# ScalarE's order inside the mixers' slots: key merges before the output tile, turned-weight copies before the next exponentials

## What is computed

```python
# mixer 1, per head: a chunked scan with decays (forward and backward)
A = jnp.einsum('bhtk,bhsk,bhtsk->bhts', qc, kc, decay)
o = einsum('bhts,bhsv->bhtv', A, vc) + einsum('bhtk,bhkv->bhtv', qc * exp(b), S)
# mixer 2, per head: differential attention over blocks of 128 queries
p = jax.nn.softmax(s, axis=-1)
a = p[:, :, 0] - lam * p[:, :, 1]
return jnp.einsum('bhqk,bhkv->bhqv', a, v)
```

## Time and profile before

| what | value |
|---|---|
| median of 3 runs | 2445.93 us (2445.45 to 2447.43) |
| profiled execution, its own time | 2445.96 us |
| its span | 2444.1 us |
| TensorE busy | 2428.1 us (99%) |
| VectorE busy | 1825.5 us (75%) |
| ScalarE busy | 1302.2 us (53%) |
| mixers of layer 0 and of layer 1 | from 240 to 503 us and from 1451 to 1714 us |

### The profile page before, as it was taken

One profiled execution on the slowest core, in us unless ns is written; L12 is line 12 of the kernel. 1 busy time (PEld: TensorE's weight loads), 2 busy tenths in 40 slices (PEclk: granted clock), 3 DMA queues, 4 the chain that ended last, 5 costly groups with the idle time before them and its releaser, 6 DMA issues.

```text
span 2444.1 us, 40830 instructions
## 1 busy us (share of the span) xinstructions
PE 2428.1 (99%) x16442; PEld 2259.2 (92%) x16442; DVE 1825.5 (75%) x2395; ACT 1302.2 (53%) x2006; POOL 189.3 (8%) x236
## 2 busy tenths in 40 slices
PE   9999999999999999999999999999999999999998
PEld 9999889898999999888899998989989999998887
DVE  6665777754788998978585567776648889999784
ACT  6444666543465555556454456664435565554563
POOL 0001011100200000003110011111002000000031
PEclk9999999999999999999999999999999999999999
DMA  5454444254323333833233544433443222346421
GB/s 177 141 173 142 133 144 134 97 184 152 104 71 90 90 104 105 300 114 128 97 130 124 187 134 140 136 122 123 174 146 110 65 89 83 107 160 247 154 92 61
DMA packets 290267, 321.52 MB, mean 132 GB/s; under 512 B 10400, under 2 KB 223904, under 8 KB 290080
## 3 DMA queue, kind: packets, MB, share of 16 engines
q1 hardware_dynamic: 215744, 171.39, 22.5%
q10 hardware_dynamic: 74336, 147.53, 16.6%
HBM read 253.60 MB, written 65.27 MB: 130 GB/s over the span
## 4 chain that ended last, share of the span: by engine, by line
PE 95%; DVE 2%; ACT 2%; issue 1%; POOL 0%; ACTq 0%; DVEq 0%; POOLq 0%
PE ps L849 21%; PE ps L1115 14%; PE ps L1297 13%; PE ps L1062 10%; PE ps L822 5%; PE ps L1403 5%; PE ps L1045 5%; PE ps L1266 3%; PE ps L1233 3%; PE ps L836 3%; PE ps L1015 2%; PE ps L901 1%; PE ps L1383 1%; PE ps L1034 1%; PE ps L958 1%; PE ps L995 1%
## 5 line engine op out<-in xcount | busy, mean ns | idle before, releaser
L849 PE MATMUL ps<-hT_hi,whi 128*128 128x384 f32 x608 | 203.7, 335 | 2.9 <-issue 1.3
L849 PE MATMUL ps<-hT_lo,whi 128*128 128x384 f32 x608 | 203.1, 334 | 0.0
L849 PE MATMUL ps<-hT_hi,wlo 128*128 128x384 f32 x608 | 203.1, 334 | 0.0
L2004 DVE TENSOR_TENSOR wlo<-raw,whi 128x1024 fp32r<-128x1024 f32 (+1 forms) x154 | 165.5, 1074 | 48.6 <-ACT whi L2964 48.6
L2979 ACT ACTIVATE U<-ps 128x384 f32<-128x384 f32 x152 | 74.7, 492 | 219.4 <-PE ps L849 219.4
L1297 PE MATMUL ps<-whi,PH_hi 128*128 128x512 f32 x456 | 179.0, 393 | 0.5 <-issue 0.4
L1297 PE MATMUL ps<-whi,PH_lo 128*128 128x512 f32 x456 | 177.7, 390 | 0.0
L1297 PE MATMUL ps<-wlo,PH_hi 128*128 128x512 f32 x456 | 177.5, 389 | 0.0
L1481 DVE TENSOR_TENSOR wlo<-raw,whi 128x2048 fp32r<-128x2048 f32 x53 | 122.2, 2306 | 67.8 <-ACT whi L2324 67.8
L1609 DVE TENSOR_TENSOR wlo<-raw,whi 128x1024 fp32r<-128x1024 f32 (+1 forms) x98 | 102.8, 1069 | 79.5 <-ACT whi L2492 79.4
L2964 ACT ACTIVATE whi<-raw 128x1024 fp32r<-128x1024 f32 (+1 forms) x154 | 143.7, 933 | 18.3 <-PE ps L901 9.6
(11 more groups left out here) (322 smaller groups left out, 7004.4 us busy)
## 6 DMA issues: line engine op xcount, KB each, us to landing
raw<-w_up_dram SPq DMA_DIRECT2D x88, 512.0 KB
raw<-w_in_dram SPq DMA_DIRECT2D x64, 512.0 KB
raw<-w_down_dram SPq DMA_DIRECT2D x60, 512.0 KB, 4.8
raw<-w_in_dram SPq DMA_DIRECT2D x16, 1024.0 KB
zT<-gst ACTq DMA_DIRECT2D x40, 384.0 KB, 2.4
GT<-zT ACTq DMA_DIRECT2D x16, 768.0 KB, 5.8
pD<-CG ACTq DMA_DIRECT2D x26, 384.0 KB, 2.3
zT<-hn ACTq DMA_DIRECT2D x48, 192.0 KB, 1.8
```

Of the source, the lines that this page charges most:

```text
L849: ins = mm(ps[:, 4 * (j % 2) + bank, 0:TH], quarter(L, W[y], j, (w,))[:, 0, k * P:(k + 1) * P], sum_operand(a, x, k), start=(opens and k = ...
L2004: v.tensor_tensor(quarter(L, wlo, j, names), raw_quarter(j, names), quarter(L, whi, j, names).bitcast(F32), ALU.subtract)\
```

## The change

In each slot ScalarE's order changes from

copy_out, `oc{k-1}`, `km{k+1}`, store_out, `nb/e{k+1}`, `at{k}`, high

to

copy_out, `km{k+1}`, `oc{k-1}`, store_out, `at{k}`, `nb/e{k+1}`, high.

The list of names follows. No instruction is added or removed, and the other engines' programs differ only in the counter values that they wait for.

```diff
@@ att_names
-        act += ([f"oc{k - 1}"] if k else []) + ([f"nb{k + 1}", f"e{k + 1}_0", f"e{k + 1}_1"] if k + 1 < NT else []) + ([f"at{k}"] if k < NT else [])
+        act += ([f"oc{k - 1}"] if k else []) + ([f"at{k}"] if k < NT else []) + ([f"nb{k + 1}", f"e{k + 1}_0", f"e{k + 1}_1"] if k + 1 < NT else [])
@@ scalar, mixers
                     side_out(1 + k)
+                    if k + 1 < NL:
+                        merge_keys(it, k + 1)
                     if k:
                         if k == 1:
                             act.wait_ge(ab_st[1], heads_stored(L, h))
                         done(A_pe, it, f"av{k - 1}")
                         a(O2[:, k - 1, :], ps[:, AB[2], 0:P], ACT.Identity, scale=rc[:, (k - 1) % 2, 0:1]).then_inc(*A_act.step(f"oc{k - 1}"))
-                    if k + 1 < NL:
-                        merge_keys(it, k + 1)
                     side_store(1 + k)
-                    if k + 1 < NT:
-                        att_exponentials(it, k + 1)
                     if k < NT:
                         kn = SEQ_OF[k][1]
                         done(A_pe, it, f"tra{k}")
                         if k == 0 and it:
                             done(A_dve, it - 1, "ss")
                         a(At[:, k % 2, 0:kn], ps[:, AB[2], 0:kn], ACT.Copy).then_inc(*A_act.step(f"at{k}"))
+                    if k + 1 < NT:
+                        att_exponentials(it, k + 1)
                     side(1 + k)
```

## The result

The changed kernel takes 2470.59 us (2470.37 to 2472.37), against 2445.73 us of the kernel before in the same comparison: ratio 1.0103, 95% interval 1.009 to 1.0115. It is 24.9 us slower; 20.7 us were forecast (2466.7), and the range to 2475 holds it. The profiled execution took 2470.37 us with a span of 2468.5 us, 24.4 more than before.

A forecast was written before the change was run, and what follows sets the result against it. TensorE, busy 2428.1 of 2444.1 us, was taken to bound the kernel. Per layer 9.09 + 1.0 + 0.4 less 0.15 gives 10.35 us; two layers add 20.7 to 2445.96: 2466.7 us, range 2459 to 2475.

The forecast's parts named there:

- The bound: TensorE in the mixers: its idle time, all that any reordering can win, is 1.97 us, 0.08% of the time.
- The late merges: Head 0 slot 5, head 1 slot 4, head 2 slot 3, head 3 slot 2: TensorE stops 1.90 to 2.90 us, 9.09 per layer.
- The chain: Late slots: low part, scaling of keys, merge, output tile, turned weights follow each other; tile ends 1.17 us after merge's start.
- the second part: Copy of turned weights ahead of exponentials on ScalarE: wins nothing, costs nothing by itself, but closes a 6.16 us ring.
- The ring: From one turn of weights to the next, through three engines: 6.16 us; shorter slots pay, 0.4 us per layer in head 0.
- The slots 5 of heads 1 and 3: No scores there and a copy out comes first, so the turned weights come 0.47 us late in head 1; head 3 alike.
- The clock: Rival: TensorE's clock falls after the eight large stalls, 1.3 us each, 10.3 us more, 2477 us; chance 0.05.
- the rivals: Clock falls after a stall (2477 us), ring binds everywhere (2478), no cost (down to 2444.0); chance 0.05 each.
- all eight stalls: The large TensorE waits at turned weights, four late merges in each of two layers, 1.9 to 2.9 us each.
- likeliest case: Eight large and some ten small stalls in the mixers, 2466.7 us, own range 2461.5 to 2471; chance 0.85.
- the forecast's own upper end: 2471 us: every reaction 0.05 us longer and the ring 6.4 us, 2 us more per layer.
- What the profile should show: Eight large turned-weight waits, 18 us in all; merge idle time at the same places; mixer stretches each 10 us longer.

The follow-up runs named there:

- the merge alone: Kernel before with only the merge moved ahead of the output tile, the exponentials staying ahead of the copy of turned weights: 2472.34 us, ratio 1.0109.
- a part ahead: Changed kernel, with TensorE doing the first side part (2.1 us) ahead of the turned weights in each layer's four late slots: 2460.96 us, ratio 1.0063.
- one late merge alone: Kernel before with the merge ahead of the output tile in one slot per layer: head 3 slot 2, 2453.34 us; head 0 slot 5, 2454.08 us.

## Why the prediction was right, and where it was off

**The bound.** TensorE had 1.97 us to give in the mixers, and the copy ahead of the exponentials, which was forecast to win nothing, measured 0.9999 by itself. Right.

**The late merges.** The forecast of 9.09 us per layer measured 8.55. The chain is the one written down: putting the four back or taking the low part out of it removes the loss but for 3 to 3.5 us. The sizes were off by small things in both directions. TensorE starts 0.15 us after the tile's end (286.79 to 286.94), where 0.05 was chosen; against that the high copy, and with it all that follows, came 0.11 to 0.27 us sooner after the turning. That gain of the second part was not in the working, which called ScalarE's time before the high copy the same sum of work in either order. The work is the same, but in the order before a wait for the maximum stood in it, and the copy of turned weights now runs in that wait. The run with the merge alone showed it.

**The ring.** 6.16 us worked out from rows of a kernel in which it was not closed; measured 6.23 (265.38 to 271.61) and 6.22 in head 0. The turned weights of its slots 2 and 3:

```profile
265.38 0.63 PE L1025 MATMUL ps<-ident,PR 128*128 128x128 f32 x4 [0.19 <-ACT O L2600]
271.61 0.63 PE L1025 MATMUL ps<-ident,PR 128*128 128x128 f32 x4 [0.20 <-ACT O L2600]
```

The gap in slot 2 had been overlooked: there a token unit's copy out consists of two instructions ahead of merge and tile. The slots 5 of heads 1 and 3 came as forecast (0.53 for 0.47), head 2's had room.

**The clock.** This is the term that was mis-sized: the sum had 0 for it, and it measured 4.6 us. It stood among the rivals with a chance of 0.05, priced at 1.3 us a fall but for all eight stalls, 2477 or more. Each fall cost 1.5, and three of eight stalls had one. Nor was head 0's stall, the longest, the first to pay: in layer 0 it had no fall, and head 3's of 2.11 us had one. The error was to treat the clock as all or nothing and apart from the forecast, when the forecast itself named eight idle times of 1.9 to 2.9 us, of a length that no row of the kernel before held. A term of 0 to 10 us within the likeliest case (eight falls at its own 1.3 us), taken at its middle, would have been the better reading. That 2470.6 still lies below the forecast's own upper end of 2471 is luck: that end was made for longer reactions and a longer ring, and not for the clock, which brought the time there.

**What the profile should show.** The waits came where they were announced. ScalarE's idle time before merges did not stay at its old places. Its line over the whole span:

```profile
  DVE KS L1658: 74.1, 28
```

74.1 us in 28 places against 35.2 in 14. Of the seven new places in a layer, two are in head 0, slots 3 and 4, and are the ring that costs 0.2 us each there. Behind the other five TensorE has no gap above 0.03 us: the merge meets its wait before the bank is wanted. The mixer stretches grew by 11.8 and 13.4 us instead of 10 each; one fall is in the first and two are in the second.

**What stays open** is which stall brings a fall. In the changed kernel and with the merge alone, stalls of 1.8 us had none (four), of 1.9 us one in four, of 2.1 to 2.4 three in four, of 2.85 and more two in four. With a part ahead the stalls of 2.05 us had one in two, and with one late merge alone four of four had one. More than the length counts, and no run here varied what that might be. Each of these counts comes from one trace per kernel.

## What to carry to other kernels

An instruction in an engine's order takes over the waits of what is put ahead of it. Before such a move, list the idle time before the moved instruction place by place. A mean hides it: most merges before were not late at all, and four waits of some 2 us in each layer, made by VectorE's low part, carry nearly the whole result. Then look at who is waiting for the one overtaken, and when: here it released a PSUM bank that TensorE wants 1.6 us into the slot (341.36 to 342.98 us in the earlier trace rows).

Useful work moved ahead of a late wait hides it only if what waits behind is not in a ring as long as the slot. And a stall of TensorE can cost more than its length: in the traces here the clock fell with 11 of the 18 stalls of 1.9 to 3.0 us that were left unfilled, for 1.4 to 1.6 us more each time.

## What the runs showed of the hardware

The granted clock fell to 0.50 with idle times of 1.92 us at the shortest, and did not fall with one of 2.98 us (the merge alone, layer 1). The same stream of instructions had a fall in one layer and none in the other layer of one execution. In the changed kernel the falls began at the stall's end in layer 0 (within 0.03 us; 468 to 469 us still shows 1.00) and 0.7 and 1.1 us behind it in layer 1, so that the price was paid on useful products. It is not always so: with one late merge in head 3, layer 1's stall lasts until 1678.05 us, and the clock is already down in the window before its end:

```profile
1677.00:1678.00 1.00, 0.00 (x0) 0.00 (x0) 1.00 (x2) 0.96 (x3) 0.00 (x0) 0.86 0.74 214
```

That fall, begun some 0.3 us before the end of the stall, was the cheapest, 1.4 us. With dummy products through the stall no fall came in any of the eight places, of which three had one without them.

TensorE's first product started 0.15 us after the end of the ScalarE instruction that released it (286.79 to 286.94 us); ScalarE started 0.03 us after its releaser on VectorE or TensorE (285.66 to 285.69 us, 287.57 to 287.60, where TensorE's end is a modelled one).
